# Three staggered stages in the scan loop of a state-space mixer

## The reference

```python
bu_re = einsum('blgc,gpc->blgp', ug, bb_re)      # and bu_im
# h[t] = lam * h[t-1] + bu[t], complex, along the sequence (associative_scan)
y = einsum('blgp,gcp->blgc', h_re, c_re) - einsum('blgp,gcp->blgc', h_im, c_im) + d_skip * ug
z = gelu(y) @ ssm_w_glu
```

## Time and profile before

| | us |
|---|---|
| median of six runs | 5624.24 |
| lowest, highest | 5598.27, 5712.47 |
| profiled execution | 5592.54 |
| its span on the slowest core | 5591.0 |
| busy in it: PE, DVE | 3681.3, 3391.4 |
| busy in it: ACT, POOL | 903.9, 695.4 |

### The profile page before, as it was taken

How to read it: one execution, slowest core, us unless ns; L and a number is a source line. 1 busy time by engine, 2 the same in 40 slices (tenths; PEclk the granted TensorE clock), 3 DMA queues, 4 the chain that set the end, 5 groups by cost and what they waited for, 6 DMA issues and landing times.

```text
span 5591.0 us, 78592 instructions; the slowest of 8 cores (5565.4 to 5591.0 us)
## 1 busy us (share of the span) xinstructions
PE 3681.3 (66%) x22072; PEld 2142.9 (38%) x22072; DVE 3391.4 (61%) x10642; ACT 903.9 (16%) x2155; POOL 695.4 (12%) x1137
## 2 busy tenths in 40 slices
PE   1389985688885688886588884831111148889986
PEld 0255542455542355542355542410000024445553
DVE  4344453577763577764477776578888864454445
ACT  1311102200002200002200001211111123321112
POOL 2100000000000000000000000046666630000000
PEclk9699996699997699987599997855555568989997
DMA  4712203122101311100412112000000033331111
GB/s 37 117 18 35 29 12 59 44 35 27 21 12 28 76 29 24 29 12 8 95 18 35 26 16 31 1 1 1 1 1 1 1 81 110 131 56 28 30 23 61
DMA packets 173238, 195.41 MB, mean 35 GB/s; under 512 B 54224, under 2 KB 140240, under 8 KB 172816
## 3 DMA queue, kind: packets, MB, share of 16 engines
q0 software_dynamic: 133472, 103.30, 13.9%
q1 hardware_dynamic: 39344, 87.10, 4.8%
HBM read 285.27 MB, written 15.73 MB: 54 GB/s over the span
## 4 chain that ended last, share of the span: by engine, by line
PE 52%; DVE 23%; issue 12%; DMA 5%; POOL 4%; ACT 2%; DVEq 1%; SPq 1%; POOLq 0%; ACTq 0%
PE ps L512 14%; PE ps L507 14%; PE ps L478 11%; DVE hT L482 7%; PE ps L633 4%; DVE xn L454 2%; PE ps L787 2%; DVE rstd L452 2%; PE ps L642 1%; PE ps L583 1%; PE ps L447 1%; DMA WS<-cw_scr 1%; DVE junk_7 L547 1%; PE ps L804 1%; DMA xst_59<-xs 1%
## 5 line engine op out<-in xcount | busy, mean ns | idle before, releaser
L482 DVE SCALAR_TENSOR_TENSOR hT<-ps,hT 128x344 f32<-128x344 f32 x1920 | 908.2, 512 | 239.2 <-PE ps L478 235.6
L512 PE MATMUL ps<-xn,WS 128*128 128x344 bf16 x5280 | 896.3, 313 | 21.2 <-DVE actb_123 L518 4.6
L507 PE MATMUL ps<-xn,WS 128*128 128x344 bf16 x5280 | 900.7, 314 | 0.0
L512 PEld LDWEIGHTS ps<-xn,WS 128*128 128x128 bf16 x5280 | 523.7, 99 | 289.4 <-issue 22.8
L507 PEld LDWEIGHTS ps<-xn,WS 128*128 128x128 bf16 x5280 | 516.3, 99 | 233.0 <-issue 0.2
L491 POOL DMA_DIRECT2D WS<-ffn_w_gate x40 | 36.2, 906 | 2979.6 <-PE ps L507 2296.1
L722 PE MATMUL ps<-Hh_183,CPad 128*128 128x172 bf16 x192 | 43.9, 309 | 340.4 <-POOL Hh_183 L677 340.4
L722 PE MATMUL ps<-Hh_182,CPad 128*128 128x172 bf16 x192 | 42.7, 311 | 338.7 <-POOL Hh_182 L677 338.7
L594 DVE COPY hT<-ps 128x512 f32<-128x512 f32 (+1 forms) x68 | 45.1, 664 | 254.2 <-PE ps L583 254.2
L547 DVE SCALAR_TENSOR_TENSOR junk_7<-ps,Es 128x172 f32<-128x172 f32 x576 | 191.2, 332 | 1.2 <-issue 1.2
L547 DVE SCALAR_TENSOR_TENSOR junk_8<-ps,Ec 128x172 f32<-128x172 f32 x576 | 190.9, 331 | 0.9 <-issue 0.4
(11 more groups left out here) (391 smaller groups left out, 6406.6 us busy)
## 6 DMA issues: line engine op xcount, KB each, us to landing
WS<-cw_scr SPq DMA_DIRECT2D x48, 896.0 KB, 4.7
WS<-ffn_w_gate POOLq DMA_DIRECT2D x30, 768.0 KB, 9.6
WS<-ffn_w_up POOLq DMA_DIRECT2D x30, 768.0 KB, 13.5
WS<-ffn_w_down POOLq DMA_DIRECT2D x30, 768.0 KB, 7.4
WS<-ffn_w_gate POOLq DMA_DIRECT2D x10, 512.0 KB, 5.9
WS<-ffn_w_up POOLq DMA_DIRECT2D x10, 512.0 KB, 8.4
...
```

The costliest lines, as they stand in the source:

```text
L482: P.dve(lambda e, dt_=dt_, pb=pb, tok=tok: e.scalar_tensor_tensor(out=hT[:, dt_, tok], in0=ps[pb][:, 0:SB], scalar=0.5, in1=hT[:, dt_, tok ...
L507: P.pe(lambda e, kc=kc, fi=fi, par=par, sl=sl, tok=tok: e.matmul(ps[par][:, 0:SB], lhsT=wsg[sl][:, kc, fi * 128:(fi + 1) * 128], rhs=xn[:, ...
L512: P.pe(lambda e, kc=kc, fi=fi, par=par, sl=sl, tok=tok: e.matmul(ps[2 + par][:, 0:SB], lhsT=wsu[sl][:, kc, fi * 128:(fi + 1) * 128], rhs=x ...
```

## The change

The body of the pair loop is cut into three functions of the pair's number i, from 0 to 191. `st1` is the input matmuls, t1 to t4, `wre` and `wim`. `st2` is the two scans and the copies to `glast`, and for the chunk's last pair also the carry update. `st3` is d1 to d4, both halves of `Hh` and, for every fourth pair, the output matmuls, the skip term and the gelu. A new loop calls them for three different pairs in one round. The operations, tiles, buffer sets and PSUM banks are the same as before.

```diff
-                    npc = 0
-                    for c in range(NT // TC):
-                        for gp in range(16):
...
+                    def ctx(i):
+                        c, gp = divmod(i, 16)
+                        return dict(c=c, gp=gp, ct=gp // 4, b=i % NBUF, pbk=i % NBUF, tk=slice(c * TC, (c + 1) * TC),
+                                    s_=(c * TC) // SB, hb=(c * 4 + gp // 4) % 2)
+                    def st1(i):
...
+                        P.pool(TTf(X("wre"), X("t1"), X("t2"), ALU.add), r=[K("t1"), K("t2")], w=[K("wre")])
+                        P.pool(TTf(X("wim"), X("t3"), X("t4"), ALU.subtract), r=[K("t3"), K("t4")], w=[K("wim")])
+                    def st2(i):
...
+                        P.act(lambda e: e.activation(out=glast[:, 1, gp:gp + 1], in_=gim_[:, TC - 1:TC], func=AF.Copy),
+                              r=[K("gim")], w=[("glast", 1, gp)])
+                        if gp == 15:
+                            gk = [("glast", ri, g_) for ri in range(2) for g_ in range(16)]
+                            P.dve(TTf(ctmp[:, 0, :], glast[:, 0, :], cosN[:], ALU.mult), r=gk + ["cosN"], w=["ctmp0"])
...
+                    def st3(i):
+                        P.pool(TTf(X("d1"), X("gre"), Ec[:, gp, :], ALU.mult), r=[K("gre"), "Ec"], w=[K("d1")])
...
+                    for i in range(NPAIR + 2):
+                        if i < NPAIR:
+                            st1(i)
+                        if 0 <= i - 1 < NPAIR:
+                            st2(i - 1)
+                        if 0 <= i - 2 < NPAIR:
+                            st3(i - 2)
```

More of the change, by code:

```diff
@@ L677, in do_block @@
                     TTf = lambda o, a_, b_, op: (lambda e: e.tensor_tensor(out=o, in0=a_, in1=b_, op=op))
-                    npc = 0
-                    for c in range(NT // TC):
-                        tk = slice(c * TC, (c + 1) * TC)
-                        s_ = (c * TC) // SB
-                        for gp in range(16):
[L683 to L737, removed]
@@ new lines, in do_block @@
+                    NCH = NT // TC
+                    NPAIR = NCH * 16
+                    def ctx(i):
[3 more added lines that the diff above has]
+                    def st1(i):
+                        q = ctx(i); gp, ct, b, pbk, tk, s_ = q["gp"], q["ct"], q["b"], q["pbk"], q["tk"], q["s_"]
+                        PA, PB = ps[pbk][:, 0:TC], ps[pbk][:, TC:2 * TC]
+                        K = lambda n_: (n_, b)
+                        X = lambda n_: T[(n_, b)][:]
+                        P.pe(lambda e: e.matmul(PA, lhsT=BqPad[:, gp, 0, :], rhs=uT[:, ct, tk], start=True, stop=True),
+                             r=["BqPad", ("uT", ct, s_)], w=[psk(pbk)])
+                        P.pe(lambda e: e.matmul(PB, lhsT=BqPad[:, gp, 1, :], rhs=uT[:, ct, tk], start=True, stop=True),
+                             r=["BqPad", ("uT", ct, s_)], w=[psk(pbk)])
+                        P.dve(TTf(X("t1"), PA, Ec[:, gp, :], ALU.mult), r=[psk(pbk), "Ec"], w=[K("t1")])
+                        P.dve(TTf(X("t2"), PB, Es[:, gp, :], ALU.mult), r=[psk(pbk), "Es"], w=[K("t2")])
+                        P.dve(TTf(X("t3"), PB, Ec[:, gp, :], ALU.mult), r=[psk(pbk), "Ec"], w=[K("t3")])
+                        P.dve(TTf(X("t4"), PA, Es[:, gp, :], ALU.mult), r=[psk(pbk), "Es"], w=[K("t4")])
+                        P.pool(TTf(X("wre"), X("t1"), X("t2"), ALU.add), r=[K("t1"), K("t2")], w=[K("wre")])
+                        P.pool(TTf(X("wim"), X("t3"), X("t4"), ALU.subtract), r=[K("t3"), K("t4")], w=[K("wim")])
@@ new lines, in st3 @@
+                    def st3(i):
+                        q = ctx(i); gp, ct, b, tk, s_, hb = q["gp"], q["ct"], q["b"], q["tk"], q["s_"], q["hb"]
+                        K = lambda n_: (n_, b)
+                        X = lambda n_: T[(n_, b)][:]
+                        P.pool(TTf(X("d1"), X("gre"), Ec[:, gp, :], ALU.mult), r=[K("gre"), "Ec"], w=[K("d1")])
+                        P.pool(TTf(X("d2"), X("gim"), Es[:, gp, :], ALU.mult), r=[K("gim"), "Es"], w=[K("d2")])
+                        P.pool(TTf(Hh[hb][:, gp % 4, 0, :], X("d1"), X("d2"), ALU.subtract), r=[K("d1"), K("d2")], w=[("Hh", hb, gp % 4, 0)])
+                        P.dve(TTf(X("d3"), X("gre"), Es[:, gp, :], ALU.mult), r=[K("gre"), "Es"], w=[K("d3")])
+                        P.dve(TTf(X("d4"), X("gim"), Ec[:, gp, :], ALU.mult), r=[K("gim"), "Ec"], w=[K("d4")])
+                        P.dve(TTf(Hh[hb][:, gp % 4, 1, :], X("d3"), X("d4"), ALU.add), r=[K("d3"), K("d4")], w=[("Hh", hb, gp % 4, 1)])
+                        if gp % 4 == 3:
+                            for k in range(8):
+                                gl, ri = k // 2, k % 2
+                                P.pe(lambda e, gl=gl, ri=ri, k=k: e.matmul(
+                                    ps[4 + hb][:, 0:TC], lhsT=CPad[:, ct * 4 + gl, ri, :], rhs=Hh[hb][:, gl, ri, :],
+                                    start=(k == 0), stop=(k == 7)),
+                                    r=["CPad", ("Hh", hb, gl, ri)], w=[psk(4 + hb)])
+                            P.dve(lambda e: e.scalar_tensor_tensor(
+                                out=ya[hb][:], in0=uT[:, ct, tk], scalar=dsk[:, ct:ct + 1], in1=ps[4 + hb][:, 0:TC],
+                                op0=ALU.mult, op1=ALU.add), r=[psk(4 + hb), ("uT", ct, s_), "dsk"], w=[("ya", hb)])
+                            P.act(lambda e: e.activation(out=ga[:, ct, tk], in_=ya[hb][:], func=AF.Gelu_apprx_tanh),
+                                  r=[("ya", hb)], w=[("ga", ct, s_)])
```

17 lines of the change are left out of this document (added).

## The result

The changed kernel takes 5584.47 us (median of 8 runs, 5534.11 to 5664.83); the kernel before, run beside it, takes 5647.53 us (median of 16 runs). The ratio is 0.987, with a 95% interval of 0.9811 to 0.9929. The forecast was 5562 us, 41 us less than before, in a range of 5530 to 5606.

The account below looks back on a forecast made before the run. DVE and POOL, taking turns at SBUF reads, were taken to bound the state-space stage. Terms -40 - 2 + 0 + 1 = -41 us took 5592.54 to 5551.5; adding 11 gave 5562, range 5530 to 5606.

Parts of the forecast that it names:

- Step 1: Each round: wait before gre goes, but SBUF reads taking turns return part; 0.21 us shorter (0.15 to 0.28), -40 us.
- single signs: In the changed trace: wim 0.70 to 0.86 us, gim 0.76 to 0.89, d3 0.61, d4 0.68, idle before gre near zero.
- Step 2: Carry update at 12 chunk ends: some 0.4 us wait for ACT's copy, offset by overlap; +5 to -5, taken as -2 us.
- Step 3: At 48 group ends: DVE's 0.59 us wait for PE before the skip addition stays; 0 us.
- Step 4: Filling and draining: two rounds at each end hold only part of the work; 0 to 2 us, taken as 1.
- (a): Rounds: the whole wait before gre comes back, -67 us, 5536 us in a run; chance 0.13.
- (b): Rounds: ten SBUF reads served one after another, each held to its operation's end; gain 0, 5602 in a run; chance 0.17.
- (c): Group ends: POOL's Hh comes behind DVE's, 0.51 us longer before 48 skip additions, +24.5 us; chance 0.08.
- this last term: Whole time: 11 us added to 5551.5, as the middle of the lowest three runs lies above the profiled execution.

Follow-up runs that it names:

- the late additions: Against the changed kernel: wre and wim one round behind t1 to t4, scans and all that follows two rounds behind; ratio 0.9794, stage 770.2 us.
- the late tail: Against the changed kernel: scans back in their own pair's round, only d1 to d4 and Hh one round late; ratio 0.9943, stage 837.4 us.
- the repeat: The changed kernel timed once more with no edit; ratio 0.9908, stage 826.9 us, profiled execution 5546.38 us.

## Why the prediction was right, step by step

**Step 1, the wait and the turns, was right in its mechanism; its size was too small.** The forecast took 0.21 us a round from the span 0.15 to 0.28; measured is 4.25 - 4.00 = 0.25 between the middles of the rounds, and 192 x 0.25 = 48 us in place of 40, inside 29 to 54. The term that was off is how long a scan holds POOL off. The forecast let it lie between 0.34 and 0.47 us. The scans of the late additions show its lone length, 0.56 us, so in the changed kernel gre got through at 4004.53 + 0.65 - 0.56 = 4004.62, and wim, 0.54 alone, at 4004.77 + 0.76 - 0.54 = 4004.99: the scan held 0.37 us. gim got through at 4005.11 + 0.79 - 0.54 = 4005.36, again 0.37 behind wim. That is 1.08 us behind t4, where 1.04 to 1.17 were forecast and 1.32 stood before. From there to the next t1 it is 4007.57 - 4005.36 = 2.21 us, the 2.23 of before: nothing changed behind gim, as forecast. The single signs came out too: wim 0.76 (0.70 to 0.86, where the forecast's own terms give 0.73 for the lower end), gim 0.79 (0.76 to 0.89), d3 and d4 at 0.61 and 0.68 as before, no idle time in front of gre.

**Step 2, the carry update, had the wrong sign.** Each part was seen (0.45 us of wait for about 0.4, d3 at 0.33 for about 0.3), but the six small instructions were costed at the 0.74 us that they take with POOL idle. They have two inputs in SBUF, and now POOL runs d2 and its `Hh` beside them: 1.29 us. A round with a chunk's end takes 4029.41 - 4024.48 = 4.93 us, 0.93 more than its neighbours, where the carry update added 0.74 before: 12 x 0.2 = +2 us in place of -2. Both lie inside the +-5 that the step allowed.

**Step 3, the group ends, was right:** the skip addition waits for PE as long as before. **Step 4** cannot be read apart: 48 - 2 - 1 is 45, and the stages give 46.9 and 47.6; a rounding of 0.01 us in a round is worth 2 us.

**The rivals.** (a), that all 67 us come back, falls with wim and gim at 0.76 and 0.79 us, and with the kernel of the late tail, which keeps the wait and has 37 of the 47 us. (b), that nothing comes back, falls with gre: it ends at 4005.18, and had it waited for wre's end (4004.81) it would have ended at 4005.37. (c) falls with the 0.60 us before the skip addition.

What (b) took as its rule is a sentence of the Trainium skill, page "SBUF — State Buffer", section "Summary: rules for kernel authors": of a DVE instruction with two SBUF inputs and a GpSimd instruction that reads SBUF, the second to issue blocks until the first finishes. (The section that the forecast names with it, "Who interferes with whom", has the contention itself.) The experiments agree that the two exclude each other and that an operand in PSUM takes the DVE instruction out of it (0.30 us for d3 beside a running d1), but they let the second in after 0.36 to 0.37 us of an instruction of 0.54 to 0.56, and here the measurement decides.

**The time itself.** The profiled execution of before, 5592.54, less 47 is 5545.5, and the repeat's profiled execution took 5546.38. The median of the changed kernel's runs, 5584.47, lies 39 us above 5545.5, where the forecast had added 11; this last term was too small by 28 us, far more than the gain was off. The kernel before varies in the same way, with a median of 5624.24 earlier and of 5647.53 beside these runs. That the median still fell into the range of 5530 to 5606 is in part luck, and says little of the mechanism: with the 11 us added, no gain at all (5603.5) would have lain in it too. What bears the mechanism out is the stage, forecast at about 833 us and measured at 827, and the single signs in it.
